# Hybrid decoder step: the output projection third by third, parts of two norms ahead of their stages, and a later load of the output weights

## What is computed

```python
def swiglu_ffn(x, g, w_gate, w_up, w_down):
    h = rmsnorm(x, g)
    return (jax.nn.silu(h @ w_gate) * (h @ w_up)) @ w_down

# layer
x = x + 0.5 * swiglu_ffn(x, n_ffn1, ...)
z = rmsnorm(x, n_mix) @ w_in          # q, three k/v pairs, gates, pooling input
x = x + concat(NSA(z), MultiScalePool(u)) @ w_out
x = x + 0.5 * swiglu_ffn(x, n_ffn2, ...)
y = rmsnorm(x, n_final)
```

## Time and profile before

| | us |
|---|---|
| median of 3 runs | 2938.79 |
| lowest, highest run | 2934.41, 2942.31 |
| the profiled execution | 2937.25 |
| its span | 2935.4 |
| TensorE busy | 2684.3 |
| VectorE busy | 1470.2 |
| ScalarE busy | 887.7 |
| GpSimd busy | 387.1 |

### The profile page before, as it was taken

How to read it: one execution, slowest core, us unless ns; L and a number is a source line. 1 busy time by engine, 2 the same in 40 slices (tenths; PEclk the granted TensorE clock), 3 DMA queues, 4 the chain that set the end, 5 groups by cost and what they waited for, 6 DMA issues and landing times. The chain is left out here.

```text
span 2935.4 us, 45571 instructions
## 1 busy us (share of the span) xinstructions
PE 2684.3 (91%) x17676; PEld 2522.6 (86%) x17676; DVE 1470.2 (50%) x2860; ACT 887.7 (30%) x1570; POOL 387.1 (13%) x432
## 2 busy tenths in 40 slices
PE   4899988999999999999968888677999999999997
PEld 4898987999999999978956666456989999999997
DVE  4444446444444444454147767554274444444445
ACT  4656555111111111032246656343141111111112
POOL 3444430000000000000012221451000000000001
PEclk9999999999999999999969989798999999999999
DMA  4131314211111110031321001486031111111101
GB/s 175 63 123 62 123 64 143 65 43 43 43 43 43 43 43 29 1 112 42 99 63 44 33 34 44 180 269 208 11 98 44 43 43 43 47 53 43 50 15 60
DMA packets 166269, 207.10 MB, mean 71 GB/s; under 512 B 11215, under 2 KB 147280, under 8 KB 163371
## 3 DMA queue, kind: packets, MB, share of 16 engines
q1 hardware_dynamic: 154834, 142.81, 15.8%
q0 software_dynamic: 11296, 62.45, 5.8%
HBM read 191.39 MB, written 18.01 MB: 71 GB/s over the span
## 5 line engine op out<-in xcount | busy, mean ns | idle before, releaser
L409 ACT ACTIVATE f_act_gate<-f_act_gate 128x352 f32<-128x352 f32 x132 | 65.8, 498 | 1186.0 <-DVE f_act_gate L483 1186.0
L500 DVE SCALAR_TENSOR_TENSOR trunk<-f_down,trunk 128x352 f32<-128x352 f32 x528 | 275.6, 524 | 208.3 <-PE f_down L104 208.3
L102 PE MATMUL f_up<-f_h_hi,f_gu_hi 128*128 128x352 f32 x1056 | 344.5, 326 | 0.0
L102 PE MATMUL f_gate<-f_h_hi,f_gu_hi 128*128 128x352 f32 x1056 | 344.3, 326 | 0.0
L104 PE MATMUL f_up<-f_h_hi,f_gu_lo 128*128 128x352 f32 x1056 | 342.7, 325 | 0.0
L104 PE MATMUL f_gate<-f_h_hi,f_gu_lo 128*128 128x352 f32 x1056 | 342.5, 324 | 0.0
L102 PE MATMUL f_down<-f_a_hi,f_wd_hi 128*128 128x352 f32 x1056 | 341.0, 323 | 0.0
L103 PE MATMUL f_gate<-f_h_lo,f_gu_hi 128*128 128x352 f32 x1056 | 340.5, 322 | 0.0
L103 PE MATMUL f_up<-f_h_lo,f_gu_hi 128*128 128x352 f32 x1056 | 340.1, 322 | 0.0
L103 PE MATMUL f_down<-f_a_lo,f_wd_hi 128*128 128x352 f32 x1056 | 338.5, 321 | 0.0
L104 PE MATMUL f_down<-f_a_hi,f_wd_lo 128*128 128x352 f32 x1056 | 338.1, 320 | 0.0
(11 more groups left out here) (374 smaller groups left out, 5414.1 us busy)
## 6 DMA issues: line engine op xcount, KB each, us to landing
f_gu_raw<-in_w_ffn_gate_dram SPq DMA_DIRECT2D x44, 512.0 KB, 4.2
f_gu_raw<-in_w_ffn_up_dram SPq DMA_DIRECT2D x44, 512.0 KB, 5.7
f_wd_raw<-in_w_ffn_down_dram SPq DMA_DIRECT2D x22, 1024.0 KB, 5.0
as_pages<-in_cache_kv_slc_dram SPq DMA_DIRECT2D x128, 128.0 KB, 3.5
as_pages<-in_cache_kv_slc_dram POOLq DMA_DIRECT2D x128, 128.0 KB, 3.5
at_spread<-saved_rows SPq DMA_DIRECT2D x16, 768.0 KB, 4.0
x_saved<-trunk SPq DMA_DIRECT2D x2, 2112.0 KB, 13.2
trunk<-x_saved SPq DMA_DIRECT2D x3, 1408.0 KB, 7.8
```

Of the source, the lines that this page charges most:

```text
L102: pe.matmul(out, w_hi, x_hi, start=first, stop=False)
L409: act.activation(act_gate[:, b, :], act_gate[:, b, :], ACT.Silu).then_inc(silu_done, 1)
L500: dve.scalar_tensor_tensor(xT[:, m, chunk(c)], down_bank[n % 4][:, 0:CH], 0.5, xT[:, m, chunk(c)], ALU.mult, ALU.add).then_inc(down_free, 1)
```

## The change

Four places, tied to one another by tiles that now outlive a stage (they are placed at the other end of SBUF, `side="right"`):

- *Input projection's norm ahead.* In the last pair of the first feed-forward, ScalarE makes the high parts and squares of third 0 and the high parts of third 1, VectorE puts one low part of third 0 behind each update of third 1 and five low parts of third 1 behind updates of third 2 (`LOWS_AHEAD = 5`), TensorE does total 0 behind the first down unit of third 2, in a free gate bank. SP loads the gain and, behind the last weight split, the first 1 MB of w_in. The feed-forward's down weights now land in the tile for w_in; the squares lie in the free tile of gate and up weights.
- *Input projection.* ScalarE begins with the high parts of the first weights, then third 2; TensorE with units, the totals 1 and 2 behind the third and the fourth of them.
- *Output weights behind pages.* SP waits for the last page of both rings, then issues the four loads.
- *Output projection.* Thirds outside, blocks inside; all eight weight blocks have split tiles of their own, and are split during the first third. SP's loads are interleaved: x 0, weights 4, 5, 6, x 1, weights 7, x 2. During thirds 1 and 2 the second feed-forward's norm is made for thirds 0 and 1 whole (high, square, total, root, low, invert), into the tiles of the mixer's parts. Behind the eighth unit SP loads the feed-forward's first gate and up weights.
- *Second feed-forward* starts with the split of the gate half, then of the up half, of weights that are there; only third 2 of the norm is left, its total behind the second third's units.

```diff
+        if ahead:
+            wd_raw = next_w[:].rearrange("p k n -> p (k n)")[:, 0:2 * D_MODEL].rearrange("p (s n) -> p s n", s=2)
+            spare = gu_raw_both[:].rearrange("p s j k n -> p (s j k n)")
+            next_norm.sq = spare[:, 0:KT * CH].rearrange("p (k n) -> p k n", k=KT)
+            next_norm.tmp = spare[:, KT * CH:(KT + 1) * CH]
...
+        def wait_third(engine, c):
+            engine.wait_ge(up_done, UNITS * PAIRS + ONE)
+            engine.wait_ge(down_free, DOWNS * (PAIRS - 1) + KT * (c + 1) + 4)
...
+                if not prepared:
+                    norm.load(sp, gain)
+                    load_gu(0, 0, 0)
...
+                if ahead:
+                    next_norm.load(sp, next_gain)
+                    sp.wait_ge(wd_split, PAIRS + ONE)
+                    sp.dma_start(next_load[0], next_load[1]).then_inc(next_landed, 16)
+                    sp.wait_ge(next_norm.gain_in, 16)
...
+                if prepared:
+                    for j in range(2):
+                        high_first(j)
+                    norm.high(act, xT, h_hi, 2)
+                    norm.square(act, xT, 2)
...
+                if ahead:
+                    for s in range(2):
+                        act.wait_ge(gu_split[s], PAIRS + ONE)
+                    wait_third(act, 0)
+                    next_norm.high(act, xT, h_hi, 0)
+                    next_norm.square(act, xT, 0)
+                    wait_third(act, 1)
+                    next_norm.high(act, xT, h_hi, 1)
+                    next_norm.root(act, 0)
...
+                def prepared_lows():
+                    for j, (high, low) in enumerate(((gate_hi_done, gate_split), (gu_hi_done[0], gu_split[0]))):
+                        dve.wait_ge(high, 1)
+                        dve.tensor_tensor(gu_lo[0][:, j], gu_raw[0][:, j], gu_hi[0][:, j].bitcast(F32),
+                                          ALU.subtract).then_inc(low, 1)
+                    norm.low(dve, xT, h_hi, h_lo, 2)
+
+                if prepared:
+                    prepared_lows()
...
                         if first and c == 1:
+                            if prepared:
+                                norm.mean_square(dve, sum_bank, 2)
                             norm.invert(dve, 2)
...
+                            if last and ahead and c == 1:
+                                next_norm.low(dve, xT, h_hi, h_lo, 0, range(m, m + 1))
+                            if last and ahead and c == 2 and m < LOWS_AHEAD:
+                                next_norm.low(dve, xT, h_hi, h_lo, 1, range(m, m + 1))
+                                if m == 3:
+                                    next_norm.mean_square(dve, gate_bank[0], 0)
...
+                if not prepared:
+                    norm.total(pe, sum_bank, 0)
+                    norm.total(pe, sum_bank, 1)
...
+                        if first and prepared and j == 0 and c == 0:
+                            pe.wait_ge(gu_split[0], 1 + ONE)
...
+                        if first and s == 0 and prepared:
+                            pe.wait_ge(gate_split, 1)
+                        else:
+                            pe.wait_ge(gu_split[s], i + 1 + ONE)
...
+                            if first and s == 0 and c == (1 if prepared else 0):
                                 norm.total(pe, sum_bank, 2)
...
+                            if last and ahead and (c, m) == (2, 0):
+                                pe.wait_ge(pair_free, UNITS * PAIRS + 2)
+                                next_norm.total(pe, gate_bank[0], 0)
...
-                norm.load(sp, gain)
-                load(0)
                 load(1)
...
+                    if i == 0:
+                        act.wait_ge(first_landed, 16)
...
-                norm.square(act, trunk, 0)
-                norm.high(act, trunk, h_hi, 0)
+                high(0)
+                norm.high(act, trunk, h_hi, 2)
                 norm.square(act, trunk, 1)
-                high(0)
-                norm.root(act, 0)
-                norm.high(act, trunk, h_hi, 1)
                 norm.square(act, trunk, 2)
-                norm.high(act, trunk, h_hi, 2)
                 norm.root(act, 1)
                 norm.root(act, 2)
                 high(1)
...
-                norm.low(dve, trunk, h_hi, h_lo, 0)
-                norm.mean_square(dve, sum_bank, 0)
                 low(0)
-                norm.low(dve, trunk, h_hi, h_lo, 1)
+                norm.low(dve, trunk, h_hi, h_lo, 1, range(LOWS_AHEAD, KT))
+                norm.low(dve, trunk, h_hi, h_lo, 2)
                 norm.invert(dve, 0)
+                take_u(0, 0, 0)
                 norm.mean_square(dve, sum_bank, 1)
-                norm.low(dve, trunk, h_hi, h_lo, 2)
-                take_u(0, 0, 0)
                 norm.invert(dve, 1)
                 norm.mean_square(dve, sum_bank, 2)
                 take_u(0, 0, 1)
...
-                norm.total(pe, sum_bank, 0)
+                u_unit(0, 0, 0)
+                u_unit(0, 0, 1, True)
+                u_unit(0, 0, 2, True)
                 norm.total(pe, sum_bank, 1)
-                u_unit(0, 0, 0, True)
+                u_unit(0, 1, 0)
                 norm.total(pe, sum_bank, 2)
-                for m, c in ((0, 1), (0, 2), (1, 0), (1, 1), (1, 2)):
-                    u_unit(0, m, c)
+                u_unit(0, 1, 1)
+                u_unit(0, 1, 2)
...
                 w_view = w_out.rearrange("(k p) (m n) -> p m k n", p=P, n=P)
-                for m in range(len(w_out_raw)):
-                    sp.dma_start(w_out_raw[m][:], w_view[:, m]).then_inc(w_out_landed[m], 16)
+                for landed in (pages_landed, more_landed):
+                    sp.wait_ge(landed[(PAGES - 1) % RING], 16 * GP * SHARE * (PAGES // RING))
+                for m in range(len(w_out_landed)):
+                    sp.dma_start(w_out_raw[:, m], w_view[:, m]).then_inc(w_out_landed[m], 16)
...
+        spare = w_raw_all[:].rearrange("p i k n -> p (i k n)")
+        norm.sq = spare[:, 0:KT * CH].rearrange("p (k n) -> p k n", k=KT)
+        norm.tmp = spare[:, KT * CH:(KT + 1) * CH]
...
+                norm.load(sp, gain)
+                load_x(0)
+                load_w(4)
+                load_w(5)
+                load_w(6)
+                load_x(1)
+                load_w(7)
+                load_x(2)
+                sp.wait_ge(done, KT)
+                for target, source in next_loads:
+                    sp.dma_start(target, source).then_inc(next_landed, 16)
+                sp.wait_ge(norm.gain_in, 16)
...
                 high(0)
-                for c in range(CHUNKS):
-                    high_mix(c)
-                for m in range(1, KT):
+                high_mix(0)
+                high(1)
+                high(2)
+                high_mix(1)
+                high(3)
+                high(4)
+                high_mix(2)
+                for m in range(5, KT):
                     high(m)
+                act.wait_ge(w_split, KT)
+                for c in range(2):
+                    act.wait_ge(added, KT * (c + 1))
+                    norm.high(act, xT, mix_hi, c)
+                    norm.square(act, xT, c)
+                    norm.root(act, c)
...
+                low(0)
+                low_mix(0)
+                low(1)
+                low(2)
+                low_mix(1)
+                low(3)
+                low(4)
+                update(0, 0)
+                update(0, 1)
+                low_mix(2)
+                for m in range(2, KT):
+                    update(0, m)
+                    if m + 3 < KT:
+                        low(m + 3)
                 for m in range(KT):
-                    if m + 1 < KT:
-                        low(m + 1)
-                    for c in range(CHUNKS):
-                        n = CHUNKS * m + c
-                        if m == 0:
-                            dve.wait_ge(x_in[c], 16)
-                        dve.wait_ge(done, n + 1)
-                        dve.tensor_tensor(xT[:, m, chunk(c)], xT[:, m, chunk(c)], banks[n % 4][:, 0:CH],
-                                          ALU.add).then_inc(added, 1)
+                    update(1, m)
+                    dve.wait_ge(done, KT)
+                    norm.low(dve, xT, mix_hi, mix_lo, 0, range(m, m + 1))
+                norm.mean_square(dve, sum_bank, 0)
+                for m in range(KT):
+                    update(2, m)
+                    if m == 0:
+                        norm.invert(dve, 0)
+                    if m < 4:
+                        dve.wait_ge(done, 2 * KT)
+                        norm.low(dve, xT, mix_hi, mix_lo, 1, range(2 * m, 2 * m + 2))
+                    if m == 4:
+                        norm.mean_square(dve, sum_bank, 1)
+                        norm.invert(dve, 1)
...
-                for m in range(KT):
-                    pe.wait_ge(w_split, m + 1)
-                    for c in range(CHUNKS):
-                        n = CHUNKS * m + c
```

(52 more changed lines are left out.)

157 lines of the change are left out of this document (92 added, 65 removed).

## The result

The changed kernel takes 2917.68 us (median of 4 runs, 2909.90 to 2920.31), the kernel before 2937.51 us beside it: ratio 0.9933, 95% interval 0.9919 to 0.9947. That is 19.8 us less; 10.1 were forecast and 2921 was the lower end of the range. The profiled execution of after is the fastest of its runs, 2909.90 us (span 2907.3).

The account below looks back on a forecast made before the run. TensorE, busy 91% of the span, was taken as the bound. Gains of 8.7 + 0.5 + 0.9 = 10.1 us took the profiled 2937.25 us to 2927.2, a median of 2928.7 us; range 2921 to 2938.

Parts of the forecast that it names:

- seams: Gains between first feed-forward and input projection (8.7 us), at sample attention's end (0.5), between output projection and second feed-forward (0.9).
- the clock's restart: After a stage's end TensorE comes back at 1.2 GHz; forecast cost 2.2 us per restart, ends 1.5 and 2.9.

Follow-up runs that it names:

- e5: Kernel before plus a measurement behind its end: 29 operand placements, 120 matmuls each; copies of real placements ran at 159.25 to 162.0 ns a matmul.
- e9: Kernel before plus a measurement behind its end: 16 cases, inputs and weights each 0, 32, 64 or 96 bytes past multiples of 128; 159.8 to 162.1 ns.
- e3: The changed kernel run again, unchanged, as a control; 2917.71 us, ratio 0.9930 to the kernel before.
- e4: The changed kernel without the two waits for pages in front of the four output weight loads; 2919.81 us.
- e6: The changed kernel with the output projection of the kernel before and its second feed-forward's norm and placement; 2922.99 us, ratio 0.9958 to the kernel before.
- e7: The changed kernel with four pads of 64 to 96 bytes, aligning feed-forward and projection operands to 128 bytes; 2903.77 us, ratio 0.9894 to the kernel before.

## What to carry to other kernels

A change that allocates tiles elsewhere is a change of every matmul that reads them: compare matmuls per us in a stretch without idle time (counts at the same busy time and clock) before crediting seams. For matmuls of this form keep weights and inputs at the same address modulo 128 bytes, and above all avoid inputs 96 ahead of the weights; pads of under 100 bytes gave 13 to 18 us in the old kernel and 11 to 14 in the new one (by ratios and by medians). A transfer that is needed later should not be asked for while the path waits for small ones of another queue: here the small ones took 5.0 to 5.7 us to land in place of 2.9 to 3.4. And one execution is too few to tell in which order two queues moved their bytes: here it showed 0.29 MB where six others had 1.0 to 1.7.

## What the hardware showed beyond expectation

- The pace of these 352-column matmuls at clock 1.00 lies between 158.94 and 163.3 ns in the kernels and repeats to 0.03 ns between executions. By the placement of their operands alone it goes from 159.0 to 162.2 ns (e5, e9).
- The difference of inputs and weights modulo 128 explains the steps at 160 and 162 ns. It does not explain what is left: with difference 0 the pace was 158.94 to 159.7 in the aligned kernels, 160.0 in the second feed-forward's down units of after, 159.0 to 159.25 in e5 and 159.8 to 159.9 in e9. Nor why after's output projection ran at 163.3 ns where the same placement alone gave 162.0. This stays open.
- What the clock's restart costs changes from one execution to the next: behind the same gap of 3.37 us the first unit of the projection lost 1.8 us in after, 2.7 in e3, which is the same kernel, 2.8 and 2.9 in e4 and e6, and 0.2 in e7.
